# The second block's mixer in another order: ScalarE splits weights one unit ahead and empties whole tiles, GpSimd makes the rotation tables

## The chip, the core and the metric

One core of one Trainium2 chip. The metric is the device time of one execution in microseconds.

## The reference

Two transformer blocks of different kinds run one after the other on 256 tokens of width 1024, each with two layers, all in fp32. The change touches the mixer of the second block:

```python
h = rms_norm_2(x, attn_norm)
proj = h @ w_in                                     # 1024 x 5444
aq, ak, av, iq, ik, iw, bq, bk, bv, gates = split_cols(proj)
aq, ak, bq, bk = (apply_rope(rms_norm_2(., gain), cos, sin)) # per head of 64
iq = apply_rope(iq);  ik = apply_rope(rms_norm_2(ik, idx_k_norm))
ya = sparse_attention(aq, ak, av, iq, ik, iw, k_sel)         # 64 best keys by relu(iq.ik), 8 heads
yb = diff_attention(bq, bk, bv, lam)                         # 4 heads, p1 - lam * p2
merged = sigmoid(g_a) * (ya @ w_up_a) + sigmoid(g_b) * (yb @ w_up_b)
x = x + merged @ w_out
```

## The kernel before

Every large product runs as three passes of TensorE in a rounded fp32 format: w_hi with aT_hi, w_lo with aT_hi, w_hi with aT_lo (`three`, lines 1703 to 1705). Weights come in **units** of 128 x 2048 elements (1 MB). For each unit SP issues two loads into `raw` (line 402), ScalarE writes the rounded part `w_hi` (`split`, line 647) and VectorE the rest `w_lo` (line 1055). There are four slots: SP's load of unit u waits until VectorE has split unit u-4, ScalarE's split of u until TensorE has used u-4, and TensorE's use of u until VectorE has split it.

The second mixer's input projection has 11 **tiles** of 512 columns (the first has 324), listed in `WIN2`; tile n is units 2n and 2n+1, `P2_WIN + 2 * n + j` in the code, so that units 14 to 21 are `P2_WIN + 14` to `+ 21`. `full_k` runs a tile: for each unit, token half i = 0, then i = 1, four groups of three matmuls each, 16 groups a tile, numbered 0 to 15. `tile_half` is raised when the first token half of the tile is complete (group 11), `units_used` with the last group. The results are in two PSUM banks, one for each token half; the first four tiles alternate between banks 0, 1 and 2, 3, and from tile 4 on all use 0 and 1 (`BANK2`). A tile's first matmul in a bank waits in `free_banks` (line 2115) until the bank has been emptied. Tiles 0 to 6 are emptied by `evac`: ScalarE takes token half 0 (line 879), VectorE token half 1 (line 1444). Tiles 7 to 10 hold the gates, and VectorE adds their bias on the way out (`gate`, line 1454).

Between the groups TensorE does the attention's small work, at places written out by hand in the functions `beside_...` (lines 2191 to 2279): `turn` transposes the rotated projections (line 1822), `index_scores` and `pair_qk` are score products (lines 2135 and 2148), `pair_turn` transposes probabilities (line 2161), `diff_pv` and `sparse_pv` multiply them with the values (lines 2171 to 2173 and 2186). Pairs 0 to 3 are the differential heads, pairs 4 to 7 the sparse ones.

For each projection that is normalized per head, ScalarE squares (`head_squares`, line 888), VectorE sums (`head_sums`, line 1465), ScalarE takes roots (`head_roots`, line 901), VectorE the reciprocal (`head_scales`, line 1473), and GpSimd rotates (`rotate2`, lines 588 to 604), five times in a layer. The rotation reads tables `rg`, gain times cosine or sine, which VectorE makes in `gain_tables` (line 1422): those of the index key ahead of tile 0, the other four behind the first `head_sums`. `item` copies the transposed projections out of PSUM (lines 711 and 1128). For a pair k, VectorE masks the scores and takes their maximum (`masked`, line 1506), ScalarE takes exponentials (`exps`, line 919), VectorE scales (`probs`, lines 1514 to 1528), TensorE transposes, and `probs_turned` copies out (lines 930 and 1536). `index_relu` and `index_score` (lines 911 and 1482) make the score of the key selection, and 8 rounds of `best` (lines 1492 and 1495) find the 64 largest.

Each engine runs its part in the order in which the program writes it, and a wait holds everything behind it on that engine. For ScalarE the list starts at line 950, for VectorE at line 1569. SP issues the loads in the order of use; the layer's small parameters come ahead of unit 0, and 1 MB of gate bias is issued between units 3 and 4 (line 503), after the layer's input has been squared.

A range of SBUF is shared by both blocks and by the feed-forward layers (`proj1`, `proj2`, `gT_hi` and others, closed by `region_end`). It lies behind `att`, `ident`, `causal`, `score` and other small tensors.

## Time and profile before

| | us |
|---|---|
| median of 3 runs | 1948.23 (1947.63 to 1948.25) |
| the profiled execution's own time | 1948.37 |
| its span, first to last instruction | 1946.5 |
| second block, layer 0, tile 1's first matmul | 1109.24 |
| scores of pair 0 | 1160.93 |
| layer 0, VectorE's evacuation of tile 6 (half 1) | 1213.76 |
| layer 0, VectorE's last gate evacuation | 1279.00 |
| mean granted TensorE clock | 0.983 |

All times of a row count from the span's start. "Idle before" in brackets is how long the engine stood still, with the instruction that ended it. A clock of 1.00 is 2.4 GHz and 0.50 is 1.2 GHz.

### The profile page before, as it was taken

What the parts mean: (1) busy time and instruction counts of PE and PEld (TensorE: products, weight loads), DVE (VectorE), ACT (ScalarE), POOL (GpSimd) and SP (SyncE); (2) the same over time, 40 slices, a digit from 0 to 9 for tenths busy, and PEclk for the clock granted to TensorE, in tenths of its full rate; (3) what the DMA queues carried; (4) which work ended last, traced back from release to release, by engine and by line L of the source; (5) the groups of instructions that cost most, each with busy time, mean ns of one, the idle gap of its engine ahead of it and who ended that gap; (6) DMA issues with size and microseconds to landing.
All of it is one profiled execution on the core that took longest, in us unless ns stands there. A gap on an engine that the chain in (4) does not pass through costs nothing.

```text
span 1946.5 us, 25911 instructions
## 1 busy us (share of the span) xinstructions
PE 1828.4 (94%) x8739; PEld 1471.2 (76%) x8739; DVE 1137.0 (58%) x1710; ACT 924.2 (47%) x1249; POOL 174.7 (9%) x186
## 2 busy tenths in 40 slices
PE   6999999999989999999999787899999788899999
PEld 5888777788868887777888666687888666687887
DVE  5554677654445545776544587675554676665552
ACT  5444475544344434755443544544443544545441
POOL 0000110000000001100000183000000363000000
PEclk9999999999999999999999899999999999999999
DMA  7555362555446554625554343355545433355551
GB/s 230 182 194 203 130 193 66 173 185 201 158 153 191 184 210 132 190 70 173 176 202 165 147 155 109 109 174 180 187 173 187 153 130 109 130 195 161 184 190 69
DMA packets 221031, 316.49 MB, mean 163 GB/s; under 512 B 14048, under 2 KB 162160, under 8 KB 220656
## 3 DMA queue, kind: packets, MB, share of 16 engines
q1 hardware_dynamic: 220912, 315.02, 49.0%
q8 instruction: 60, 0.98, 0.2%
q14 instruction: 59, 0.48, 0.1%
HBM read 313.93 MB, written 1.05 MB: 162 GB/s over the span
## 4 chain that ended last, share of the span: by engine, by line
PE 75%; DVE 8%; ACT 7%; issue 4%; DVEq 4%; ACTq 1%; SPq 0%; DMA 0%
PE ps L1703 23%; PE ps L1705 23%; PE ps L1704 23%; ACT w_hi L647 3%; DVE w_lo L1055 2%; PE ps L1789 1%; ACT att L919 1%; DVEq L1515 1%; DVEq L1457 1%; ACT aT_hi L671 1%; PE ps L1713 1%; PE ps L1822 1%; DVE aT_lo L1075 1%; PE ps L1876 1%; PE ps L1852 1%
## 5 line engine op out<-in xcount | busy, mean ns | idle before, releaser
L1055 DVE TENSOR_TENSOR w_lo<-raw,w_hi 128x2048 fp32r<-128x2048 f32 x298 | 676.0, 2293 | 278.8 <-ACT w_hi L647 277.2
L1703 PE MATMUL ps<-w_hi,aT_hi 128*128 128x512 f32 (+2 forms) x1760 | 708.4, 403 | 53.7 <-DVE aT_lo L1075 31.7
L1705 PE MATMUL ps<-w_hi,aT_lo 128*128 128x512 f32 (+2 forms) x1760 | 687.1, 390 | 0.0
L1704 PE MATMUL ps<-w_lo,aT_hi 128*128 128x512 f32 (+2 forms) x1760 | 686.2, 390 | 0.0
L647 ACT ACTIVATE w_hi<-raw 128x2048 fp32r<-128x2048 f32 x298 | 557.2, 1906 | 171.1 <-PE ps L1705 166.9
L1703 PEld LDWEIGHTS ps<-w_hi,aT_hi 128*128 128x128 f32 x1760 | 334.3, 190 | 141.5 <-DVE aT_lo L1075 36.1
L1705 PEld LDWEIGHTS ps<-w_hi,aT_lo 128*128 128x128 f32 x1760 | 334.2, 190 | 70.0
L1704 PEld LDWEIGHTS ps<-w_lo,aT_hi 128*128 128x128 f32 x1760 | 335.2, 190 | 61.0
L686 ACT ACTIVATE att<-ps,rstd 128x256 f32<-128x256 f32 x132 | 55.3, 470 | 373.3 <-PE ps L1705 373.2
L1103 DVE SCALAR_TENSOR_TENSOR att<-ps,rstd,att 128x256 f32<-128x256 f32 x132 | 57.8, 480 | 275.6 <-ACT att L686 275.6
L1703 PE MATMUL ps<-w_hi,gT_hi 128*128 128x512 f32 x528 | 209.7, 397 | 0.0
L1705 PE MATMUL ps<-w_hi,gT_lo 128*128 128x512 f32 x528 | 208.5, 395 | 0.0
L1704 PE MATMUL ps<-w_lo,gT_hi 128*128 128x512 f32 x528 | 208.5, 395 | 0.0
L1705 PEld LDWEIGHTS ps<-w_hi,gT_lo 128*128 128x128 f32 x528 | 99.0, 187 | 24.4
L1703 PEld LDWEIGHTS ps<-w_hi,gT_hi 128*128 128x128 f32 x528 | 99.0, 187 | 23.5
L1704 PEld LDWEIGHTS ps<-w_lo,gT_hi 128*128 128x128 f32 x528 | 99.0, 188 | 23.4
L671 ACT ACTIVATE aT_hi<-ps,gain_l 128x128 fp32r<-128x128 f32 x160 | 43.4, 382 | 94.0 <-PE ps L1713 79.4
L1089 DVE SCALAR_TENSOR_TENSOR x<-ps,x 128x512 f32<-128x512 f32 x40 | 25.7, 685 | 86.6 <-PE ps L1705 86.6
L563 POOL COPY tt<-proj 128x512 f32<-128x512 f32 x4 | 4.5, 1162 | 679.8 <-DVE proj L1196 679.8
L1075 DVE SCALAR_TENSOR_TENSOR aT_lo<-ps,gain_l,aT_hi 128x128 fp32r<-128x128 f32 x160 | 43.7, 343 | 33.3 <-ACT aT_hi L671 33.3
L919 ACT ACTIVATE att<-att,neg_max 128x128 f32<-128x128 f32 x64 | 28.6, 448 | 72.3 <-DVE neg_max L1506 69.7
L749 ACT ACTIVATE att<-att,neg_max 128x128 f32<-128x128 f32 x96 | 43.0, 448 | 31.7 <-DVE neg_max L1225 27.5
(245 smaller groups left out, 1334.4 us busy)
## 6 DMA issues: line engine op xcount, KB each, us to landing
raw<-in_w_in SPq DMA_DIRECT2D x120, 512.0 KB, 4.4
raw<-in_w_ffn_gate SPq DMA_DIRECT2D x88, 512.0 KB, 4.2
raw<-in_w_ffn_up SPq DMA_DIRECT2D x88, 512.0 KB, 5.2
raw<-in_w_ffn_down SPq DMA_DIRECT2D x88, 512.0 KB, 4.4
raw<-in_w_ffn_in SPq DMA_DIRECT2D x88, 512.0 KB, 4.9
raw<-in_w_ffn_out SPq DMA_DIRECT2D x44, 512.0 KB, 4.4
raw<-in_w_out SPq DMA_DIRECT2D x32, 512.0 KB, 4.6
raw<-in_w_ck SPq DMA_DIRECT2D x8, 512.0 KB, 4.0
```

The source lines that it names most:

```text
L647: nc.scalar.activation(dst, src, ACT.Copy).then_inc(units_hi, 1)
L671: o = nc.scalar.activation(aT_hi[:, 4 * g + c, tok], bank[:, c], ACT.Copy, scale=gain_l[:, gain, 4 * g + c:4 * g + c + 1])
L686: o = nc.scalar.activation(sil[:, b % 2, i], ps[:, 2 * (b % 2) + i, 0:256], ACT.Silu, scale=rstd[:, i:i + 1])
L749: nc.scalar.activation(pair_p[:, k % 2, e, c:c + n], pair_p[:, k % 2, e, c:c + n], ACT.Exp, bias=pair_max[:, k % 2, e, i:i + 1], scale=-1. ...
L919: nc.scalar.activation(pair_p[:, k % 2, e, c:c + n], pair_p[:, k % 2, e, c:c + n], ACT.Exp, bias=pair_max[:, k % 2, e, i:i + 1], scale=-1. ...
L1055: V.tensor_tensor(o, a, h, ALU.subtract).then_inc(units_split, 1)
L1075: o = V.scalar_tensor_tensor(aT_lo[:, 4 * g + c, tok], bank[:, c], gain_l[:, gain, 4 * g + c:4 * g + c + 1], hi[:, c], ALU.mult, ALU.subtract)
L1089: o = V.scalar_tensor_tensor(xs, ps[:, src[i][n], :], scale, xs, ALU.mult, ALU.add)
L1103: o = V.scalar_tensor_tensor(gg[:, b % 2, i], ps[:, 2 * (b % 2) + i, 256:512], rstd[:, i:i + 1], sil[:, b % 2, i], ALU.mult, ALU.mult)
L1703: M(o, ah, wh, start=start, stop=False)
L1704: M(o, ah, wl, start=False, stop=False)
L1705: return M(o, al, wh, start=False, stop=stop)
```

## The change

The tensors from `att` to `factor` are allocated behind the shared region, so that this one follows `aT_lo`. GpSimd makes all five sets of rotation tables, ahead of its first rotation. ScalarE's `evac` takes both token halves, and one semaphore, `tile_done`, stands for a whole tile. ScalarE's splits of units 3 and on stand one place earlier in its list, the evacuation of tile 4 stands behind `exps(1)`, and VectorE's list follows the new order: splits one place earlier up to unit 16, `item(5)` ahead of a round of `best`. Behind unit 16's split VectorE's list stays as it was. TensorE's small work moves by a few groups in tiles 4 to 6.

```diff
@@
                 nc.gpsimd.tensor_tensor(a[:, i], a[:, i], lanes(scale[0][:, i, :], DH), ALU.mult)
             nc.gpsimd.drain()
+    pool.wait_ge(x_ready, 2 * 8)
+    pool.wait_ge(rope_sin, 2)
+    pool.wait_ge(params2_loaded, (l + 1) * 128)
+    for n in (2, 3, 4, 0, 1):
+        g = par2[:, 64 * n:64 * n + 64]
+        for k, (trig, half) in enumerate(((0, 0), (1, 1), (0, 1), (1, 0))):
+            nc.gpsimd.tensor_tensor(rg[:, n, k], cs2[:, trig],
+                                    heads(g[:, 32 * half:32 * half + 32], 2), ALU.mult)
+    nc.gpsimd.drain()
+
     for q, (n, c0, m0, g) in enumerate(HEAD_NORMS):
-        pool.wait_ge(proj_act, l * 7 + (12 + n + 1))
-        pool.wait_ge(proj_dve, l * 11 + (12 + n + 1))
+        pool.wait_ge(tile_done, l * 11 + (n + 1))
         if q == 0:
             rotate2(1536, 4, [cs2[:, 0], cs2[:, 1], cs2[:, 0], cs2[:, 1]])
         w = 1 if q == 0 else 8
@@
     B = l * STAGES2 + STAGES1 * L
     stage(B, 0)
     split(st, 1)
-    X, W, T = l * 2 + 7, l * 11 + 12, l * TJ2 + TJ1 * L
+    X, W, T = l * 2 + 7, l * 11, l * TJ2 + TJ1 * L
     J, O = l * PAIRS2 + PAIRS1 * L, l * 2 + 4 * L
     norm(X)
@@
         act.wait_ge(tile_half, l * 11 + (12 + n + 1))
         nc.scalar.activation(proj2[:, 0, c0:c0 + m], ps[:, BANK2[n][0], 0:m], ACT.Copy,
                              scale=rstd[:, 0:1]).then_inc(proj_act, 1)
+        act.wait_ge(units_used, st.used(P2_WIN + 2 * n + 1))
+        nc.scalar.activation(proj2[:, 1, c0:c0 + m], ps[:, BANK2[n][1], 0:m], ACT.Copy,
+                             scale=rstd[:, 1:2]).then_inc(tile_done, 1)
     def head_squares(q):
         n, c0, m0, _ = HEAD_NORMS[q]
         nc.scalar.drain()
-
-        act.wait_ge(proj_dve, W + (n + 1))
         if q != 0:
             nc.scalar.activation(squares2.rearrange("p (i n) -> p i n", i=2),
@@
             .then_inc(gates2_ready, 1)
     win_split(1, 0)
+    root(X)
     win_split(1, 1)
-    root(X)
+    win_split(2, 0)
     evac(0)
     head_squares(0)
+    head_roots(0)
     act.wait_ge(lam_sums, l + 1)
     nc.scalar.activation(lam[:, 0:2], lam[:, 0:2], ACT.Exp).then_inc(lam_exp, 1)
-    win_split(2, 0)
-    head_roots(0)
     win_split(2, 1)
+    win_split(3, 0)
     evac(1)
     head_squares(1)
-    win_split(3, 0)
+    win_split(3, 1)
     head_roots(1)
     item(0)
-    win_split(3, 1)
+    win_split(4, 0)
     index_relu(0)
     index_relu(1)
     evac(2)
     head_squares(2)
     index_relu(2)
     index_relu(3)
-    win_split(4, 0)
+    win_split(4, 1)
     head_roots(2)
     item(2)
-    win_split(4, 1)
+    win_split(5, 0)
     evac(3)
     head_squares(3)
     item(4)
-    win_split(5, 0)
+    win_split(5, 1)
     head_roots(3)
     exps(0)
-    win_split(5, 1)
+    win_split(6, 0)
+    exps(1)
     evac(4)
-    exps(1)
     probs_turned(0)
-    win_split(6, 0)
+    win_split(6, 1)
+    diff_out(0)
     exps(2)
-    diff_out(0)
     probs_turned(1)
-    win_split(6, 1)
+    split(st, P2_WIN + 14)
     exps(3)
     diff_out(1)
-    probs_turned(2)
     evac(5)
     head_squares(4)
+    probs_turned(2)
+    split(st, P2_WIN + 15)
+    head_roots(4)
     item(6)
-    split(st, P2_WIN + 14)
-    head_roots(4)
     diff_out(2)
     probs_turned(3)
-    split(st, P2_WIN + 15)
+    split(st, P2_WIN + 16)
     diff_out(3)
     evac(6)
     item(8)
-    split(st, P2_WIN + 16)
+    split(st, P2_WIN + 17)
     exps(4)
-    split(st, P2_WIN + 17)
+    split(st, P2_WIN + 18)
     exps(5)
-    split(st, P2_WIN + 18)
+    split(st, P2_WIN + 19)
     probs_turned(4)
     exps(6)
-    split(st, P2_WIN + 19)
     probs_turned(5)
+    split(st, P2_WIN + 20)
     exps(7)
+    sparse_hi(0)
+    split(st, P2_WIN + 21)
+    probs_turned(6)
     act.wait_ge(yb_ms, l + 1)
     nc.scalar.activation(ms[:, 0:8], ms[:, 0:8], ACT.Sqrt).then_inc(yb_root, 1)
-    split(st, P2_WIN + 20)
-    sparse_hi(0)
-    probs_turned(6)
-    act.wait_ge(proj_dve, W + 9)
+    split(st, P2_UP)
+    probs_turned(7)
+    act.wait_ge(tile_done, W + 9)
     gate(GATES2)
-    split(st, P2_WIN + 21)
-    probs_turned(7)
-    split(st, P2_UP)
+    split(st, P2_UP + 1)
     sparse_hi(1)
-    split(st, P2_UP + 1)
+    split(st, P2_UP + 2)
     stage(B + 4, parts=((0, 1), (1, 1)), banks=STAGE_BANKS_YB)
-    act.wait_ge(proj_dve, W + 11)
+    act.wait_ge(tile_done, W + 11)
     gate(GATES2 + DM)
-    split(st, P2_UP + 2)
     split(st, P2_UP + 3)
     split(st, P2_OUT)
@@
     stage(B, 0)
     split(st, 1)
-    def gain_tables(n):
-        g = par2[:, 64 * n:64 * n + 64]
-        for k, (trig, half) in enumerate(((0, 0), (1, 1), (0, 1), (1, 0))):
-            V.tensor_tensor(rg[:, n, k], cs2[:, trig],
-                            heads(g[:, 32 * half:32 * half + 32], 2), ALU.mult)
-
     dve.wait_ge(params2_loaded, (l + 1) * 128)
-    gain_tables(2)
     dl = par2[:, 448:704].rearrange("p (a b d) -> p a b d", a=2, b=2)
     V.tensor_tensor(score[:, 0:128].rearrange("p (a d) -> p a d", a=2), dl[:, :, 0, :], dl[:, :, 1, :],
@@
         .then_inc(lam_sums, 1)
     V.tensor_scalar(par2[:, 320:448], par2[:, 320:448], par2[:, 705:706], None, ALU.mult)
-    X, W, T = l * 2 + 7, l * 11 + 12, l * TJ2 + TJ1 * L
+    X, W, T = l * 2 + 7, l * 11, l * TJ2 + TJ1 * L
     J, O, A = l * PAIRS2 + PAIRS1 * L, l * 2 + 4 * L, l * 4 + (PAIRS1 * L - 4)
     def win_split(n, j):
         split(st, P2_WIN + 2 * n + j, 0, WIN2[n][1])
-
-    def evac(n):
-        c0, m = WIN2[n]
-        dve.wait_ge(units_used, st.used(P2_WIN + 2 * n + 1))
-        V.tensor_scalar(proj2[:, 1, c0:c0 + m], ps[:, BANK2[n][1], 0:m], rstd[:, 1:2], None,
-                        ALU.mult).then_inc(proj_dve, 1)
     def gate(n, i):
@@
             dve.wait_ge(units_used, st.used(P2_WIN + 2 * n + 1))
         V.scalar_tensor_tensor(proj2[:, i, c0:c0 + m], ps[:, BANK2[n][i], :], rstd[:, i:i + 1],
                                proj2[:, 1, c0:c0 + m], ALU.mult, ALU.add)\
-            .then_inc(proj_dve if i else gate_first, 1)
+            .then_inc(tile_done if i else gate_first, 1)
         V.drain()
@@
                 .then_inc(xn_ready, 1)
     win_split(1, 0)
+    norm(X)
     win_split(1, 1)
-    norm(X)
-    evac(0)
+    win_split(2, 0)
     head_sums(0)
-    for n in (3, 4, 0, 1):
-        gain_tables(n)
+    dve.wait_ge(tile_done, W + 1)
+    V.tensor_scalar(iw[:, 0, :], proj2[:, 0, 1856:1860], 0.5, None, ALU.mult)
+    V.tensor_scalar(iw[:, 1, :], proj2[:, 1, 1856:1860], 0.5, None, ALU.mult)
+    head_scales(0)
+    win_split(2, 1)
     dve.wait_ge(lam_exp, l + 1)
-
     V.tensor_tensor(lam[:, 2:3], lam[:, 1:2], lam[:, 0:1], ALU.subtract)
     V.drain()
     V.tensor_tensor(lam[:, 2:3], lam[:, 2:3], par2[:, 704:705], ALU.subtract)
-    V.tensor_scalar(iw[:, 0, :], proj2[:, 0, 1856:1860], 0.5, None, ALU.mult)
-    V.tensor_scalar(iw[:, 1, :], proj2[:, 1, 1856:1860], 0.5, None, ALU.mult)
-    win_split(2, 0)
-    head_scales(0)
-    win_split(2, 1)
-    evac(1)
+    win_split(3, 0)
     head_sums(1)
-    win_split(3, 0)
-    head_scales(1)
     item(1)
     win_split(3, 1)
+    head_scales(1)
+    win_split(4, 0)
     index_score(0)
     index_score(1)
-    evac(2)
+    index_score(2)
     head_sums(2)
-    index_score(2)
     index_score(3)
-    win_split(4, 0)
+    item(3)
+    win_split(4, 1)
     head_scales(2)
-    item(3)
     best(2)
-    win_split(4, 1)
-    evac(3)
+    win_split(5, 0)
     head_sums(3)
+    item(5)
     best(1)
-    item(5)
-    win_split(5, 0)
+    win_split(5, 1)
     head_scales(3)
     masked(0)
     best(1)
-    win_split(5, 1)
+    win_split(6, 0)
     probs(0)
     masked(1)
-    evac(4)
-    win_split(6, 0)
+    best(1)
+    win_split(6, 1)
     probs(1)
     masked(2)
-    best(1)
-    win_split(6, 1)
+    split(st, P2_WIN + 14)
     probs(2)
     masked(3)
-    evac(5)
+    best(1)
     head_sums(4)
+    split(st, P2_WIN + 15)
+    probs(3)
     item(7)
-    best(1)
-    probs(3)
     head_scales(4)
-    split(st, P2_WIN + 14)
     best(2)
-    split(st, P2_WIN + 15)
-    evac(6)
+    split(st, P2_WIN + 16)
     V.tensor_scalar(score[:, :], score[:, :], TAKEN, -NEG, ALU.not_equal, ALU.mult)
     V.drain()
     V.tensor_tensor(score[:, :], score[:, :], causal[:, :], ALU.add)
     V.drain()
     item(9)
-    split(st, P2_WIN + 16)
     masked(4)
     dve.wait_ge(bias_loaded, (l + 1) * 16)
@@
         def wait(i):
             if i == 1:
-                pe.wait_ge(proj_dve, W + m + 1)
+                pe.wait_ge(tile_done, W + m + 1)
             elif m < 7:
                 pe.wait_ge(proj_act, l * 7 + (12 + m + 1))
@@
             copied(3, 3)
             pe.wait_ge(idx_relu, l * 4 + 4)
             pair_qk(0)
-        if at == 12:
+        if at == 13:
             pair_qk(1)
         if at == 15:
             pair_turn(0)
     def beside_ak(at):
-        if at == 3:
+        if at == 4:
             pair_qk(2)
-            pe.wait_ge(proj_act, l * 7 + (12 + 5))
-            pe.wait_ge(proj_dve, W + 5)
+            pe.wait_ge(tile_done, W + 5)
             diff_pv(0)
-        if at == 6:
+        if at == 8:
             pair_turn(1)
-        if at == 10:
+        if at == 12:
             pair_qk(3)
             diff_pv(1)
-        if at == 13:
+
+    def beside_av(at):
+        if at == 0:
             pair_turn(2)
-
-    def beside_av(at):
-        if at == 2:
+        if at == 3:
             rotated(3)
             turn((6, 7))
             diff_pv(2)
-        if at == 5:
+        if at == 6:
             pair_turn(3)
-        if at == 10:
+        if at == 11:
             diff_pv(3)
@@
             pair_turn(4)
         if at == 10:
             pair_qk(6)
-            pe.wait_ge(proj_act, l * 7 + (12 + 7))
-            pe.wait_ge(proj_dve, W + 7)
+            pe.wait_ge(tile_done, W + 7)
             sparse_pv(4)
         if at == 14:
             pair_turn(5)
```

## Rows read from the trace of the kernel before

**Rows 1.** The page: busy time, share of the span and instructions of each engine.

```profile
PE 1828.4 (94%) x8739; PEld 1471.2 (76%) x8739; DVE 1137.0 (58%) x1710; ACT 924.2 (47%) x1249; POOL 174.7 (9%) x186
```

**Rows 2.** TensorE's waits, 1104 to 1180 us: releaser, us in total, times, longest.

```profile
PE ps L2148 <- DVE tt L1128: 4.1, 1, 4.1
PE ps L1703 <- DVE w_lo L1055: 3.4, 3, 1.9
PE ps L1822 <- POOLq L605: 2.3, 2, 1.4
PE ps L2161 <- DVE att L1528: 0.7, 1, 0.7
PE ps L1822 <- POOLq L617: 0.7, 1, 0.7
```

**Rows 3.** TensorE's waits, 1180 to 1215 us.

```profile
PE ps L2161 <- DVE att L1528: 7.5, 3, 3.1
PE ps L1703 <- ACT proj L879: 2.2, 1, 2.2
```

**Rows 4.** TensorE's waits, 1215 to 1280 us.

```profile
PE ps L1703 <- DVE proj L1454: 3.1, 2, 2.0
PE ps L2161 <- DVE att L1523: 2.1, 2, 1.9
PE ps L2186 <- DVE att L1536: 1.8, 1, 1.8
```

**Rows 5.** TensorE's waits in the second layer, 1531 to 1710 us.

```profile
PE ps L1703 <- DVE w_lo L1055: 3.5, 3, 2.0
```

**Rows 6.** Windows: length, busy PE, PEld, DVE, ACT, POOL, granted clock, DMA share, GB/s.

```profile
1104.00:1180.00 76.00, 65.12 (x308) 50.21 (x308) 63.06 (x114) 41.31 (x59) 48.76 (x39) 0.96 0.52 180
...
1215.00:1280.00 65.00, 58.01 (x289) 44.07 (x288) 39.62 (x80) 31.94 (x52) 3.54 (x4) 0.95 0.36 122
```

**Rows 7.** The same columns for one microsecond after the longest wait.

```profile
1163.00:1164.00 1.00, 1.00 (x4) 0.71 (x4) 1.00 (x5) 0.00 (x0) 1.00 (x1) 0.50 0.00 0
```

**Rows 8.** Timeline of TensorE, input tile 1: start, us, engine, line, instruction, idle before it.

```profile
1109.24 0.50 PE L1703 MATMUL ps<-w_hi,aT_hi 128*128 128x512 f32 x1 [0.29 <-DVE w_lo L1055]
...
1120.02 0.39 PE L1705 MATMUL ps<-w_hi,aT_lo 128*128 128x512 f32 x1
```

**Rows 9.** Timeline of GpSimd: first rotation, and a later one.

```profile
1112.72 0.74 POOL L588 TENSOR_TENSOR proj<-proj,cs 128x256 f32<-128x256 f32 x1 [269.57 <-DVE proj L1444]
...
1119.28 2.40 POOL L597 TENSOR_TENSOR proj<-proj 128x64 f32<-128x64 f32 x1
...
1124.83 0.40 POOL L616 COPY att<-proj 128x256 f32<-128x256 f32 x1
...
1195.36 1.29 POOL L588 TENSOR_TENSOR proj<-proj,rg 128x512 f32<-128x512 f32 x1 [27.36 <-ACT proj L879]
```

**Rows 10.** Timeline of VectorE: probabilities of pairs 0 and 1.

```profile
1171.65 0.75 DVE L1528 SCALAR_TENSOR_TENSOR att<-att,factor 128x128 f32<-128x128 f32 x2
...
1180.82 0.75 DVE L1528 SCALAR_TENSOR_TENSOR att<-att,factor 128x128 f32<-128x128 f32 x2
```

**Rows 11.** Timeline of VectorE: split of unit 17.

```profile
1226.84 2.29 DVE L1055 TENSOR_TENSOR w_lo<-raw,w_hi 128x2048 fp32r<-128x2048 f32 x1 [2.18 <-ACT w_hi L647]
```

**Rows 12.** Timeline of VectorE: rotation tables.

```profile
1113.39 5.29 DVE L1422 TENSOR_TENSOR rg<-cs,par 128x64 f32<-128x64 f32 x16
```

**Rows 13.** Timeline of VectorE: ahead of the first scores.

```profile
1157.11 1.22 DVE L1465 TENSOR_REDUCE ms<-proj 128x16 f32<-128x1024 f32 x1 [1.13 <-ACT proj L888]
...
1160.11 0.69 DVE L1128 TENSOR_SCALAR tt<-ps 128x512 f32<-128x512 f32 x1
```

**Rows 14.** Timeline of SP's DMA issues, and one window of DMA (columns as rows 6).

```profile
1105.49 18.99 SPq L402 DMA_DIRECT2D raw<-in_w_in  x11
...
1112.00:1113.00 1.00, 1.00 (x7) 0.80 (x6) 0.56 (x1) 0.87 (x4) 0.28 (x1) 1.00 1.04 399
```

**Rows 15.** Timeline of ScalarE: its half of tile 0's evacuation.

```profile
1112.02 0.53 ACT L879 ACTIVATE proj<-ps,rstd 128x324 f32<-128x324 f32 x1 [0.31 <-DVE rstd L1062]
```

More of the change, by code:

```diff
@@ L131, in build @@
         aT_lo = sb("aT_lo", [P, KC, SEQ], F32R)
-        att = sb("att", [P, 2304])
-        ident = sb("ident", [P, P])
-        causal = sb("causal", [P, 384])
-        cmask = sb("cmask", [P, 2, 16])
-        cvalid = sb("cvalid", [P, 2, 16])
-        head_mask = sb("head_mask", [P, 8])
-        gain_rows = sb("gain_rows", [80, P])
-        gain_cols = sb("gain_cols", [P, 80])
-        gain_l = sb("gain_l", [P, 3, KC])
-        ss = sb("ss", [P, 2])
-        rstd = sb("rstd", [P, 2])
-        rot1 = sb("rot1", [P, 2, 16])
-        neg_max = sb("neg_max", [P, 4, 2])
-        sums = sb("sums", [P, 4, 2])
-        with ExitStack() as r:
-            row_rot = r.enter_context(nc.sbuf_tensor("row_rot", [P, 4, 2, 8, 8], F32))
-        with ExitStack() as r:
-            score = r.enter_context(nc.sbuf_tensor("score", [P, 384], F32))
-        rot_end = sb("rot_end", [P, 512])
-        factor = sb("factor", [P, 4, 2])
         with ExitStack() as r:
@@ L177, in build @@
         region_end = sb("region_end", [P, 13800])
+        att = sb("att", [P, 2304])
+        ident = sb("ident", [P, P])
+        causal = sb("causal", [P, 384])
+        cmask = sb("cmask", [P, 2, 16])
+        cvalid = sb("cvalid", [P, 2, 16])
+        head_mask = sb("head_mask", [P, 8])
+        gain_rows = sb("gain_rows", [80, P])
+        gain_cols = sb("gain_cols", [P, 80])
+        gain_l = sb("gain_l", [P, 3, KC])
+        ss = sb("ss", [P, 2])
+        rstd = sb("rstd", [P, 2])
+        rot1 = sb("rot1", [P, 2, 16])
+        neg_max = sb("neg_max", [P, 4, 2])
+        sums = sb("sums", [P, 4, 2])
+        with ExitStack() as r:
+            row_rot = r.enter_context(nc.sbuf_tensor("row_rot", [P, 4, 2, 8, 8], F32))
+        with ExitStack() as r:
+            score = r.enter_context(nc.sbuf_tensor("score", [P, 384], F32))
+        rot_end = sb("rot_end", [P, 512])
+        factor = sb("factor", [P, 4, 2])
         with ExitStack() as r:
@@ L294, in build @@
         gate_first = sem("gate_first")
+        tile_done = sem("tile_done")
         rope_arg = sem("rope_arg")
@@ L2098, in _ @@
                 stage(x, x_ready, l * 2 + 7, 0)
-                T, W, A, D = l * TJ2 + TJ1 * L, l * 11 + 12, l * 5 + 10, l * 5 + 12
+                T, W, A, D = l * TJ2 + TJ1 * L, l * 11, l * 5 + 10, l * 5 + 12
                 B, J, O = l * STAGES2 + STAGES1 * L, l * PAIRS2 + PAIRS1 * L, l * 2 + 4 * L
```

## The prediction

> **What bounds the kernel now.** I read the page first, then TensorE's waits by stretch, then the timeline of all engines where they occur. TensorE is busy for 94% of the span [rows 1], so only what makes it stand still or slows its clock can be won. The change touches one stage, the second block's mixer, which runs twice. In the first layer, from 1104 to 1280 us, TensorE waits 11.2, 9.7 and 7.0 us in three stretches, 27.9 us in all [rows 2 to 4]; I call them early (to the first attention scores at 1160.9), middle (to the end of input tile 6, 1213.7) and late (tiles 7 to 10). The second layer has the same waits in the same places, as the three for weight splits, 3.5 us there and 3.4 here [rows 2, 5]. After the longer waits the granted clock falls to half, 1.2 for 2.4 GHz: it averages 0.96 early and 0.95 late [rows 6], and after the 4.10 us wait at 1156.8 TensorE still ran at half speed while busy in the row of 1163 [rows 7]. A full tile is 48 matmuls at 0.227 us, 10.9 us (first at 1109.24, last at 1120.02 plus 0.23) [rows 8].
>
> Three loops keep TensorE waiting. Early it is GpSimd's chain of rotations, the first of them 12.5 us long (1112.72 to 1125.23) [rows 9]; TensorE waited for three of them, 3.0 us in all [rows 2]. In the middle it is a loop through ScalarE and VectorE: scores masked, exponentials, ScalarE's split of a weight unit, VectorE's split of it, probabilities, the next scores. Probabilities are finished off at 1171.65 and again at 1180.82, so a turn takes 9.2 us [rows 10], while TensorE needs for a unit and what stands beside it 5.44 + about 3 us. Late, VectorE waits for ScalarE's split (2.18 us at 1226.84), since that stands behind the exponentials [rows 11].
>
> **Part 1, GpSimd makes the rotation tables.** 20 small multiplies a layer leave VectorE. 16 of them took 5.29 us behind the first head sums [rows 12]. GpSimd takes 0.74 us for a multiply four times as wide [rows 9], so 20 cost it at most 15 us. It does them before the first tile is ready, while it idles (269.57 us before its first rotation in layer 0 [rows 9]), so they lie off the path; in the code the parameters are loaded ahead of tile 0's weights. The unknown is whether they slow VectorE's 8 aT_lo at the head of layer 0, once: by nothing, or by one 0.33 us table instruction each (5.29 / 16), 3 us. I take 0, because those read PSUM and a single SBUF tensor, and the copy out of PSUM at 1160.11 took 0.69 us while GpSimd turned tile 3 [rows 13], no more than elsewhere. The address move of the shared region costs nothing: no instruction changes shape; a gain or loss would need a conflict that no row shows.
>
> **Part 2, early stretch.** ScalarE now splits units 3 and 4 ahead of evacuating tile 0. Unit 4's load goes out only at 1105.49, behind 1 MB of gate bias [rows 14], and at 0.36 to 0.40 MB per us [rows 14] the 2.1 MB are in at about 1112. So ScalarE splits it 1112 to 1113.9, then evacuates both halves (2 x 0.53 [rows 15]): GpSimd starts at 1115.0, not 1112.7. Worse, GpSimd's rotation stands still while VectorE splits. A 64-wide instruction took 2.40 us beside a split, where one of 256 took 0.74 and one of 512 took 1.29 without [rows 9]. Two such blocks lie in the 12.5 us, 8.4 without them. The rotation now runs beside the tail of unit 4's split (1.2), unit 5's (2.3) and unit 6's (2.3): 14 us, ending near 1129 instead of 1125.2. TensorE, which no longer waits 1.22 us for unit 4 and stands at that turn at 1122.8, waits 6 us (was 0.69). The second and third rotations follow 4 us later than before. What takes it back is the 4.10 us wait at 1156.8 [rows 2]: there the copy that the first scores need, at 1160.11, came behind VectorE's evacuation, ScalarE's squares (1.13 us of waiting), sums (1.22) and 1.8 us with a round of the top-k search in it [rows 13]. The change puts that copy ahead of the search round and takes the evacuation off VectorE. My walk brings the first scores to 1160.8, before 1160.9: **early, 0**. Ends: -6.6 (the 4.1 us wait and the 2.5 us lost to the slow clock behind it gone) and +4 (nothing absorbed).
>
> The Trainium skill (SBUF — State Buffer, Who interferes with whom) states that a VectorE instruction with two SBUF inputs and a GpSimd one that reads SBUF exclude each other for a whole instruction, and that one with a single SBUF input does not. The trace agrees on both: 2.40 us, and the unchanged 0.69 us copy. It speaks against splitting ahead, since each split moved into a rotation adds its full 2.3 us there; by a rule of shared bandwidth it would be about half.
>
> **Part 3, middle stretch.** ScalarE now empties both halves of tiles 4 and 5 behind exponentials 1 and 3, and the next tile needs the same banks. The loop's turn stays; between the two rows of [rows 10] the timeline has exponentials 2.2 us, ScalarE's split 1.9, VectorE's 2.3, probabilities 1.6 and masking, 0.4 to its first result. Walking it: TensorE waits at the first probabilities 2.9 (it arrives sooner, at full clock; was 0.72), at tile 5's start 2.8 (probabilities to masked 0.4, exponentials 2.2, evacuation 0.7, less the 0.5 of transposes), at the second and third none (were 2.05 and 2.36), since the turns were put 8 to 9 groups of 0.68 us apart instead of 7, at tile 6's start 4.8 (was 2.22 [rows 3]), at the fourth 0.9 (was 3.09): 11.4 us against 9.7 + 0.72. The 0.7 us of faster first scores and the low clock, one fall before and one or two after, about cancel: **middle, 0**, between -4 and +6.
>
> **Part 4, late stretch.** From the fifth pair's scores on, VectorE's order is as before, but ScalarE has every unit split beforehand: splits 17 to 21 move ahead of the exponentials. VectorE is busy for 39.6 of the 65 us [rows 6], which leaves room for a stretch of 56; what it lost was the wait for ScalarE [rows 11]. In the walk each of the five waits of [rows 4] goes (the nearest, the last probabilities, comes within 0.6 us of TensorE's need). Gone with them is the low clock: 0.05 of 65 us is 3.2 us, of which some 2.3 fell on a busy engine [rows 6]. **Late, -7.0 - 2.3 = -9.3**. Ends: -1.9 (only the last wait goes) and -10.2. What is late next is TensorE alone.
>
> Queues: SP's issues of weight units wait for VectorE's split four units back, all of which come at least as early except unit 3's (its split ends 2.3 us later, since the root goes ahead of it; TensorE needs it at 1114.7, it is there at 1113.7, and unit 7's load, queued behind it, is needed 10 us later). Table loads: the root for head 0 saves one and head 1 pays it, 1.28 us, hidden in TensorE's first wait. ScalarE's seven added evacuations are 4.6 us (7 at about 0.66) in an engine that is 47% busy [rows 1]; where it waits for a tile's end, the next split stands behind it, which part 3's walk holds. The upper projections and the rest keep their order and start 9 us sooner.
>
> **The sum.** 2 x (0 + 0 - 9.3) = -18.6 against the profiled execution's own 1948.37 us (span 1946.5; its 1.9 us around the span stay), which is 0.1 above the median shown: 1929.8, so 1930.
>
> **Rivals.**
> 1. *More is won* (0.15): the rotations suffer less than I walk and early gives -5 too, 2 x 14 = -28: 1920. For it: TensorE's early waits were small except the one that goes. Against: GpSimd's chain is serial.
> 2. *Little is won* (0.17): late waits turn into others, since exponentials still wait for masks (2.62 us [rows 11]) and VectorE has no slack; 2 x -2: 1944. Against it: VectorE is 61% busy there [rows 6].
> 3. *Slower* (0.18): evacuation behind the exponentials. At tiles 5 and 6 TensorE waits 2.8 and 4.8 us, each followed by some 5 us at half clock, 2 x 2.5, and the probabilities' waits do not shrink in return: +12.6 less 9.3 a layer, +6.6: 1955. It decides where the two waits with their clock exceed 9.3 us more than the middle gives back. For it: 2.22 us at 1195.26 was this very wait [rows 3], where ScalarE's half stood behind exponentials 3.
> 4. *Nothing changes* because loops trade place (0.06): 1948.
>
> **Chances.** My case 0.44. Faster by over 0.2% (3.9 us, about what a measurement of this kernel can tell): 0.44 + 0.15 + most of rival 2, 0.73. Within: 0.09. Slower: 0.18. Range: from rival 1 with the late end, 1914, to 1951, which leaves out the far part of rival 3 and little at the bottom. Where it is faster, its own range is 1916 to 1944.
>
> **What would show it.** Right: no wait of TensorE above 1 us after tile 6 and a late clock of 1.00; a wait of 4 to 6 us for GpSimd at the first turn; none at the first scores; waits for ScalarE's evacuation at the starts of tiles 5 and 6; tables on GpSimd long before the first rotation. Wrong: the first rotation ending before 1126 (part 2), the middle longer than 59 us (part 3), or waits for probabilities or gates in tiles 8 to 10 (part 4).

## The result and the profile after

The change brings 10.2 us: 1937.41 us (median of 5 runs, 1934.76 to 1937.53) against 1947.63 (5 runs), ratio 0.9945, interval 0.9931 to 0.996. The forecast was a gain of 18.6 us, to 1930, with a range of 1914 to 1951. The profiled execution is the fastest of the five (1934.76, span 1933.0), 2.6 us below the median; so what is added up from it is to be compared with 1948.37 - 1934.76 = 13.6 us and not with 10.2.

The page, its busy times (to be read against [rows 1]):

```profile
PE 1819.7 (94%) x8739; PEld 1477.6 (76%) x8739; DVE 1118.4 (58%) x1656; ACT 935.3 (48%) x1263; POOL 191.3 (10%) x226
```

TensorE has the same 8739 matmuls and is 8.7 us less busy. That is where the reading starts: something made the matmuls themselves quicker. And 6.5 us are won before the second block begins (its tile 0 starts at 1089.27 instead of 1095.8), where no instruction was changed.

TensorE's waits in the mixer of layer 0 after (1089 to 1270 us; for [rows 2 to 4]):

```profile
PE ps L2150 <- DVE att L1526: 7.4, 2, 4.5
PE ps L1692 <- ACT proj L889: 6.4, 2, 3.7
PE ps L1811 <- POOLq L627: 4.5, 1, 4.5
PE ps L1692 <- DVE aT_lo L1086: 4.1, 2, 3.5
PE ps L2150 <- DVE att L1521: 2.4, 1, 2.4
PE ps L1692 <- DVE w_lo L1066: 2.0, 1, 2.0
PE ps L2137 <- DVE tt L1139: 1.7, 1, 1.7
PE ps L1811 <- POOLq L606: 0.2, 1, 0.2
```

The 4.1 us for aT_lo and the 2.0 for w_lo lie ahead of tile 1. Windows of the same layer, early, middle and late (columns as [rows 6]), cut at tile 1's first matmul, the first scores, the turn in tile 7 (group 2), and the first upper projection:

```profile
1103.78:1155.22 51.44, 45.08 (x206) 35.64 (x204) 38.28 (x47) 32.14 (x39) 41.13 (x34) 0.93 0.58 198
1155.22:1212.61 57.39, 43.59 (x208) 33.55 (x209) 39.40 (x101) 27.93 (x56) 23.57 (x17) 0.91 0.36 118
1212.61:1269.67 57.06, 54.68 (x281) 42.43 (x280) 34.94 (x75) 32.19 (x52) 3.51 (x4) 0.97 0.35 119
```

The kernel before, cut at the same places:

```profile
1109.24:1160.93 51.69, 43.35 (x203) 33.75 (x204) 45.57 (x73) 27.58 (x35) 41.98 (x35) 0.98 0.58 201
1160.93:1215.61 54.68, 44.23 (x208) 33.64 (x209) 38.34 (x98) 25.18 (x52) 22.97 (x17) 0.92 0.35 111
1215.61:1278.80 63.19, 56.20 (x281) 42.63 (x280) 38.17 (x77) 31.94 (x52) 2.92 (x3) 0.95 0.36 121
```

Early -0.25, middle +2.7, late -6.1. Ahead of these windows tile 0 takes 14.5 us instead of 13.4, +1.1. From tile 0's start to the first upper projection with `ya` the mixer takes 180.4 us instead of 183.0, in layer 1 180.8 instead of 182.3: 4.1 us for both. The other 9.5 lie outside the code that the diff reorders. Windows of the same 40 us of a down projection in block 1, before and after:

```profile
160.00:200.00 40.00, 40.00 (x173) 32.12 (x172) 16.78 (x8) 14.23 (x8) 0.00 (x0) 1.00 0.66 225
```

```profile
160.00:200.00 40.00, 40.00 (x178) 33.15 (x177) 16.95 (x9) 14.83 (x8) 0.00 (x0) 1.00 0.67 230
```

Both have TensorE busy for the whole 40 us at a granted clock of 1.00, and 178 matmuls pass instead of 173. Measured from one matmul's start to the next one's, the mean is 227.0 ns instead of 233.3, in each of the six down projections (264 matmuls, 61.35 us for 62.95 in the first): 1.6 us each, 9.8 in all. Only the address of their stationary operands, `gT_hi` and `gT_lo`, is new: 147584 instead of 162400, bytes within a partition. Against it stand the upper projections, whose `ya_hi` and `ya_lo` moved from 205952 to 191136: the stretch from the first to the last of their 48 matmuls a layer, with others in between, takes 17.72 us instead of 17.44.

### The profile page after: what moved, and what is told of

The parts are those of the page before. It is cut to its first block, busy times and chain, and to the rows that moved or that the text cites. A ratio compares the mean times of both kernels' runs of the same rounds, so it can differ in the third digit from the quotient of the medians.

```text
span 1933.0 us, 25923 instructions
## 1 busy us (share of the span) xinstructions
PE 1819.7 (94%) x8739; PEld 1477.6 (76%) x8739; DVE 1118.4 (58%) x1656; ACT 935.3 (48%) x1263; POOL 191.3 (10%) x226
## 4 chain that ended last, share of the span: by engine, by line
PE 77%; issue 6%; DVE 6%; ACT 5%; DVEq 3%; POOL 2%; POOLq 1%; ACTq 0%; DMA 0%; SPq 0%
PE ps L1692 24%; PE ps L1694 23%; PE ps L1693 23%; ACT w_hi L657 2%; DVE w_lo L1066 2%; PE ps L1778 1%; POOL rg L614 1%; DVEq L1513 1%; PE ps L1811 1%; ACT aT_hi L681 1%; PE ps L1702 1%; PE ps L1865 1%; DVE att L1236 1%; DVE aT_lo L1086 1%; DVEq L1483 1%
## 5 line engine op out<-in xcount | busy, mean ns | idle before, releaser
L614 POOL TENSOR_TENSOR rg<-cs,par 128x64 f32<-128x64 f32 x40 | 17.2, 467 | 471.9 <-DVE x L1416 246.9
L759 ACT ACTIVATE att<-att,neg_max 128x128 f32<-128x128 f32 x96 | 42.9, 448 | 31.8 <-DVE neg_max L1236 27.5
```

Of the source, the lines that this page charges most:

```text
L614: nc.gpsimd.tensor_tensor(rg[:, n, k], cs2[:, trig], heads(g[:, 32 * half:32 * half + 32], 2), ALU.mult)
L759: nc.scalar.activation(pair_p[:, k % 2, e, c:c + n], pair_p[:, k % 2, e, c:c + n], ACT.Exp, bias=pair_max[:, k % 2, e, i:i + 1], scale=-1. ...
```

## The experiments

The times of one group share their runs of the kernel before (median 1948.71 for `e1` to `e4`, 1948.43 for `e5` and `e7` to `e9`, 1948.83 for `e6`, `e10` and `e11`, 1948.13 for `e12`; 1947.63 beside the kernel after). A difference between kernels of two groups can be off by about 1 us for that alone.

**The parts alone.** `e1_move` is the kernel before with only the allocation moved. `e2_order` is the kernel after with the allocation of before, so the order and the tables alone. `e3_pad` is the kernel before with one line added ahead of the shared region, `e4_after_pad` the kernel after with the same line:

```diff
+        pad = sb("pad", [P, 8])
```

> The kernel before with nothing but the allocation moved, so that the shared region starts at byte 147584 of a partition instead of 162400. Theory A: the move is worth some 10 us of the 10.2 measured, since in the profile after each of the six down projections took about 1.6 us less: 1938 us, and the mixer's waits stay as they were before (4.1 us at the first scores). Rival B: addresses are worth nothing and the down projections were faster by chance in that one profile: 1947.6.

> The kernel after with the old allocation: order and tables alone. Theory A: the order gives 2 to 3 us a layer, 1943 us, and the down projections are as slow as before (matmul pitch 233 ns). Rival B: the order gives everything, 1937.4.

> The kernel before with 32 unused bytes ahead of the shared region: the region starts at 162432, a multiple of 64, instead of 162400, which is 32 more than one. Theory A1, it is the start's remainder by 64 that matters: as e1_move, 1938, pitch 227 ns in the down projections. Rival A2, it is where the region lies as a whole: 1947.6, pitch 233.

> The kernel after with 32 unused bytes ahead of the region: it starts at 147616, 32 more than a multiple of 64. Theory A1: the down projections fall back to 233 ns a matmul, 1.6 us each, and the time to about 1947 less the order's 3 to 5, 1943 as e2_order. Rival A2: it stays at 1937.

Measured: `e1_move` 1940.02, ratio 0.9951 (0.9938 to 0.9965); `e2_order` 1947.46 (11 runs), 0.9994 (0.9985 to 1.0003); `e3_pad` 1939.05, 0.995 (0.9937 to 0.9964); `e4_after_pad` 1948.66 (11 runs), 0.9998 (0.9989 to 1.0007). So 32 unused bytes are worth as much as the whole change, and put in front of the change's own region they take its gain away. The order and the tables by themselves give 1.2 us with an interval that reaches from 2.9 to -0.6, where theory A had 4 to 6. The trace of `e2_order` shows why: its late stretches take 57.1 us in both layers, as in the kernel after, but its middle stretches 59.8 and 59.7, with the clock at 0.86, where the kernel before has 54.7 and 53.6. Its middle and late windows of layer 0:

```profile
1161.73:1221.49 59.76, 47.62 (x208) 36.47 (x209) 38.39 (x101) 27.92 (x56) 23.90 (x18) 0.86 0.37 122
1221.49:1278.63 57.14, 54.76 (x280) 42.43 (x279) 34.92 (x75) 32.20 (x52) 2.74 (x3) 0.97 0.33 111
```

So the order wins some 6 us a layer late and can give nearly all of it back in the middle. The window of the down projection in `e3_pad` shows the 178 matmuls:

```profile
160.00:200.00 40.00, 40.00 (x178) 33.13 (x177) 16.95 (x9) 14.99 (x8) 0.00 (x0) 1.00 0.67 234
```

**Which address.** Three kernels put unused bytes inside the shared region of the kernel after, so that the mixer's own tensors stay where they are:

```diff
 e9_lo_off
+            r.enter_context(nc.sbuf_tensor("gap", [P, 8], F32))
             gT_lo = r.enter_context(...)
 e10_plus64
+            r.enter_context(nc.sbuf_tensor("gap_hi", [P, 16], F32))
             gT_hi = r.enter_context(...)
+            rb("gap_y", [P, 24])
             ya_hi = rb("ya_hi", [P, 4, SEQ], F32R)
 e11_hi_off
+            r.enter_context(nc.sbuf_tensor("gap_hi", [P, 8], F32))
             gT_hi = r.enter_context(...)
+            r.enter_context(nc.sbuf_tensor("gap_lo", [P, 24], F32))
             gT_lo = r.enter_context(...)
```

(`e11_hi_off` has also 24 elements ahead of `ya_hi` and 8 ahead of `ya_lo`, which puts them at remainders 0 and 32 to 256 bytes.)

> The kernel after with 32 unused bytes between gT_hi and gT_lo: gT_hi still starts at a multiple of 64 bytes, gT_lo 32 bytes past one; the mixer's tensors keep their addresses. Theory (a stationary operand that starts 32 bytes past a multiple of 64 costs its own matmul about 19 ns): of the 264 matmuls of a down projection only the third with gT_lo are slow, so the mean distance between matmuls rises from 227.0 to about 229 ns, each projection by 0.5 us and the kernel by 3.3 us; the distance in front of or behind the gT_lo matmuls is 246 ns and the others stay at 227. Rival A (the lost time belongs to the pair of tensors or to VectorE's and ScalarE's writes of them, not to the matmul's own operand): all or none of the matmuls slow down, 10 us or 0. Rival B (every stationary operand off by 32 bytes loses 6.3 ns): the gT_lo matmuls take 233.3 ns, mean 229.1, the same sum but no 246 ns in the trace.

> The kernel after with 64 unused bytes ahead of gT_hi inside the shared region, so that gT_hi and gT_lo start 64 bytes past a multiple of 128 (still a multiple of 64), and 96 bytes ahead of ya_hi and ya_lo (the stationary operands of the upper projections), so that they start at a multiple of 128; the mixer's other tensors keep their addresses. Theory (the stationary operand has to start at a multiple of 128 bytes, as the runs so far have 233 ns for ya at 32 and at 64 past one and 227 at one): the down projections' mean distance between matmuls goes from 227 to 233 ns, 1.6 us each, and that of the upper projections from 233 to 227 ns. Rival (a multiple of 64 is enough, and the ya of the run with the padded address had another reason): down projections stay at 227.

> The kernel after with gT_hi 32 bytes past a multiple of 128 and gT_lo at one (the mirror of the run with gT_lo alone off), and ya_hi at a multiple of 128 with ya_lo 32 bytes past one. In that run, of three matmuls the one during which gT_lo is loaded came after 238 ns, the one after after 227 and the third after 235, 700 ns for the three as with both off. Theory (each change of stationary operand onto or away from an unaligned tensor costs, and a triple costs 700 ns as soon as any of its operands is off): 233 ns on the mean for both gT and ya. Rival A (only gT_lo's loads count): 227 for the down projections and 233 for the upper ones. Rival B (each unaligned load costs by itself 6.3 ns): 231.2 ns for gT, 229 for ya.

`e9_lo_off` took 1947.23 us (11 runs), the whole gain gone, and its six projections have 233.3 ns a matmul. The three matmuls of a group, from its timeline:

```profile
160.31 0.40 PE L1693 MATMUL ps<-w_hi,gT_hi 128*128 128x512 f32 x1
160.55 0.40 PE L1694 MATMUL ps<-w_lo,gT_hi 128*128 128x512 f32 x1
160.78 0.39 PE L1695 MATMUL ps<-w_hi,gT_lo 128*128 128x512 f32 x1
161.01 0.40 PE L1693 MATMUL ps<-w_hi,gT_hi 128*128 128x512 f32 x1
```

With `gT_lo` alone off, the group costs 19 ns more, 700 for 681, as much as with both off. My expectation of +3.3 us was wrong, and so was that of a price for each matmul. The lost time is spread: on the mean of the six projections 239 ns behind the second matmul, while the weight load of `gT_lo` runs, 232 behind the first, 228 behind the third. `e10_plus64` (one execution, 1946.33) gave 233.3 ns for `gT` at 64 bytes further, so a multiple of 64 is not what counts; and its `ya`, now at a multiple of 128, stayed at 17.74 us from the first to the last of the 48 matmuls, so a multiple of 128 is not either, which I had expected. `e11_hi_off` (one execution, 1945.84) gave 231.2 ns for `gT`, the value of its rival B, but 233.4 for `ya`, the value of the theory where rival B had 229. So neither holds as a whole, and 231.2 beside the mirror's 233.3 fits no simple sum. Windows of `e10_plus64` and of `e11_hi_off`:

```profile
160.00:200.00 40.00, 40.00 (x173) 32.25 (x172) 16.68 (x8) 14.21 (x8) 0.00 (x0) 1.00 0.65 223
```

```profile
160.00:200.00 40.00, 40.00 (x175) 32.50 (x174) 16.33 (x8) 14.60 (x8) 0.00 (x0) 1.00 0.67 229
```

Set side by side by the remainder of the address to 256, the runs agree. At 128: `gT` at 147584 and 162432, `aT_hi` and `aT_lo` in every kernel, `ya` at 205952, all 227. At 96, 160 and 192, and `ya` at 0: 232.6 to 233.4 on the mean of each run. Remainders 64 and 224 were not tried, and 32 only for `ya_lo` beside `ya_hi` at 0 (233.4). The weights, the moving operand, stood at remainder 128 in all kernels, so "128" and "the same as the weights" are not told apart.

**What the order gives, and what takes it back.** `e5_evac_first`, `e7_tables_dve` and `e8_evac0_first` are the kernel after with one part undone or turned round:

```diff
 e5_evac_first, ScalarE
+                evac(4)
                 exps(1)
-                evac(4)
@@
+                evac(5)
                 exps(3)
                 diff_out(1)
-                evac(5)
 e8_evac0_first, ScalarE
+                evac(0)
                 win_split(2, 0)
-                evac(0)
```

In `e7_tables_dve` the loop over the five tables is gone from GpSimd, and VectorE has `gain_tables(2)` at the head of the mixer and the other four behind `head_sums(0)`.

> The kernel after, with ScalarE's evacuation of tile 4 ahead of the exponentials of pair 1 and that of tile 5 ahead of those of pair 3. Theory (the middle stretch lost what the late one won, because the evacuation stands behind exponentials, rival 3's mechanism): the waits for the evacuation at the starts of tiles 5 and 6 (2.67 and 3.74 us) fall to under 1 us each and with them the half clock behind them, some 1 to 2 us a layer; 3 to 6 us a layer, so 6 to 12 us less than the kernel after, near 1928. Rival (the loop masked, exponentials, split, probabilities sets the middle; a wait taken away at the tiles' starts comes back at the next probabilities): the two waits go, those for the first and second probabilities grow by as much, the time stays within 2 us of 1937.

> The kernel after with the rotation tables back on VectorE at their old places (one table set at the head of the mixer, four behind the first head sums). Theory of the prediction (the tables are worth nothing, since what they hold up on VectorE is covered): within 2 us of the kernel after; 5.3 us more of VectorE's time behind the first head sums hold up the scales of head 0, so the first rotation ends up to 4 us later and TensorE's first wait for GpSimd, 4.50 us, grows by that if nothing covers it. Rival (the tables are what the new order needs): the first scores come 3 us or more later in each layer, 4 to 8 us slower than the kernel after.

> The kernel after with ScalarE's evacuation of tile 0 ahead of its split of unit 4 (a weight unit of tile 2), as before. Theory of part 2 of the prediction (the split in front delays the first rotation by some 2 us, TensorE waits for it at the first turn, and later work absorbs it): TensorE's wait at the first turn falls from 4.50 us to between 2 and 3, a wait for unit 4 of up to 1.2 us comes back, and the first scores come within 1 us of where they were: within 2 us of the kernel after. Rival (the 4.50 us are simply added to the early stretch): the stretch shortens by 2 us or more in each layer, 4 us or more faster in all.

`e7_tables_dve`: 1938.1 us, 0.7 slower than the kernel after and inside its expectation; the tables are worth nothing that can be told. `e8_evac0_first`: 1936.12, 1.3 faster. The wait at the first turn did not fall to 2 or 3 us: it is 4.85 in layer 0 and 3.89 in layer 1. It ends only 0.6 and 0.8 us sooner after tile 0's start than in the kernel after, and in layer 0 TensorE comes there 1 us sooner as well; the total fits, the path to it does not.

`e5_evac_first`: 1933.23, ratio 0.9916 (0.9903 to 0.993), 4.2 us less than the kernel after (4.9 less than `e7_tables_dve`, which was measured beside it), below the 6 to 12 expected. Its waits in layer 0:

```profile
PE ps L2150 <- DVE att L1526: 10.4, 4, 3.6
PE ps L1811 <- POOLq L627: 5.6, 1, 5.6
...
PE ps L2150 <- DVE att L1521: 2.4, 1, 2.4
```

The two waits for the evacuation, 6.4 us in all, are gone, and 3.0 us came back as waits for probabilities (10.4 for 7.4) and 1.1 as a longer wait at the first turn (5.6 for 4.5). The middle stretch takes 56.5 and 57.0 us, where the two passages of the kernel after have 57.4. Its timeline of ScalarE and VectorE shows why the waits stay:

```profile
1159.46 0.40 ACT L930 ACTIVATE att<-att,neg_max 128x128 f32<-128x128 f32 x1 [3.74 <-DVE neg_max L1504]
...
1161.85 1.92 ACT L657 ACTIVATE w_hi<-raw 128x2048 fp32r<-128x2048 f32 x1 [0.24 <-issue]
...
1163.79 2.29 DVE L1066 TENSOR_TENSOR w_lo<-raw,w_hi 128x2048 fp32r<-128x2048 f32 x1 [2.46 <-ACT w_hi L657]
...
1167.00 0.75 DVE L1526 SCALAR_TENSOR_TENSOR att<-att,factor 128x128 f32<-128x128 f32 x2
```

ScalarE idles 3.74 us, takes the exponentials, and only then splits the unit, for which VectorE waits 2.46 us with the probabilities behind it. `e6_splits_first` adds to `e5_evac_first`:

```diff
+                win_split(6, 0)
                 exps(0)
-                win_split(6, 0)
                 evac(4)
+                win_split(6, 1)
                 exps(1)
                 probs_turned(0)
-                win_split(6, 1)
                 diff_out(0)
+                split(st, P2_WIN + 14)
                 exps(2)
                 probs_turned(1)
-                split(st, P2_WIN + 14)
                 evac(5)
+                split(st, P2_WIN + 15)
                 exps(3)
                 diff_out(1)
                 head_squares(4)
                 probs_turned(2)
-                split(st, P2_WIN + 15)
```

> The kernel with the evacuations of tiles 4 and 5 first (1933.2), and in it ScalarE's splits of units 12, 13, 14 and 15 each ahead of the exponentials of pairs 0, 1, 2 and 3 instead of behind them. ScalarE idles 3.74, 2.70 and 3.74 us before exponentials 0, 1 and 3 while it waits for masks. Theory (each probabilities' wait comes from the chain exponentials, ScalarE's split 1.9, VectorE's split 2.3, probabilities, so taking ScalarE's split out of the chain takes 1.9 us off each turn): TensorE's four waits for the probabilities of pairs 0 to 3 (2.89, 0.71, 3.25, 3.58 us in layer 0) fall by about 2 us each, the middle stretch from 56.5 to 50 to 53 us: 7 to 12 us less in all, 1921 to 1926. Rival (VectorE is the bound of the middle: mask, split, probabilities in a fixed order, so its split only moves to where it delays the next mask): the waits change places, within 2 us of 1933.

Measured 1927.66, ratio 0.9888 (0.9871 to 0.9904), 5.6 us less than `e5_evac_first` where 7 to 12 were expected; the middle stretch takes 54.1 us in both layers. Two of the four waits for probabilities are gone, and a new one is there:

```profile
PE ps L2150 <- DVE att L1526: 6.5, 2, 3.4
PE ps L1811 <- POOLq L627: 4.7, 1, 4.7
PE ps L2160 <- ACT att L941: 2.6, 1, 2.6
PE ps L2150 <- DVE att L1521: 2.4, 1, 2.4
```

The 2.6 us are for turned probabilities that ScalarE copies behind the exponentials of pair 3. `e12_best` takes that away, and moves `ya` to remainder 128 (191360):

```diff
                 evac(5)
+                head_squares(4)
+                diff_out(1)
+                probs_turned(2)
                 split(st, P2_WIN + 15)
                 exps(3)
-                diff_out(1)
-                head_squares(4)
-                probs_turned(2)
@@
+            rb("gap_y", [P, 56])
             ya_hi = rb("ya_hi", [P, 4, SEQ], F32R)
```

> The kernel with evacuations and splits first (1927.7), and in it two things. (a) On ScalarE the squares of head norm 4, the output of pair 1 and the turned probabilities of pair 2 go ahead of the split of unit 15 and the exponentials of pair 3, behind which TensorE waited 2.64 us for the turned probabilities, VectorE 5.47 us for the squares and GpSimd 2.90. Theory (ScalarE's order is what still holds the middle stretch): the 2.64 us go, the fourth probabilities' wait (3.15 us) falls to under 2, the middle stretch goes from 54.1 to 50 to 52 us, 4 to 8 us in all: 1920 to 1924. Rival (exponentials 3 come 1.5 us later and the fourth probabilities with them): within 1.5 us of 1927.7. (b) ya_hi and ya_lo start at 191360, 384 past a multiple of 512. So far every stationary operand at 128 past a multiple of 512 (aT, gT of four kernels, ya of two) took 227 ns a matmul, and those at 96, 160, 192 and 256 past one took 233. If the rule is the remainder to 256, the upper projections' matmuls go from 233 to 227 ns (1.2 us in all); if it is the remainder to 512, they stay at 233.

Measured 1920.09 us (1919.03 to 1921.27), ratio 0.9857 (0.984 to 0.9873): 17.3 us less than the kernel after, and faster than both. Its middle window, and its upper projections' first and last matmul:

```profile
1155.05:1204.48 49.43, 42.94 (x209) 33.45 (x210) 39.22 (x101) 28.31 (x56) 25.95 (x18) 0.93 0.45 147
```

```profile
1261.59 0.39 PE L1693 MATMUL ps<-w_hi,ya_hi 128*128 128x512 f32 x1
...
1279.03 0.40 PE L1695 MATMUL ps<-w_hi,ya_lo 128*128 128x512 f32 x1
```

The middle takes 49.4 and 51.1 us. The fourth probabilities still cost a wait of 4.5 us, more than expected. The stretch of the upper projections is back at 17.44 us, with 227.1 ns from start to start of its `ya` matmuls, so the remainder to 256 counts and not that to 512; for 96 matmuls that is 0.6 us, and not the 1.2 I had expected.

## Why the prediction was right and wrong

**The address move (part 1)** is the first step that failed. It was sized at nothing, "no instruction changes shape; a gain or loss would need a conflict that no row shows", and it carries the gain: 9.8 us in the trace less 0.6 for the upper projections, and 8.7 and 9.7 us in `e1_move` and `e3_pad`. The kernel is faster mostly for another reason than the one given. The trace of the kernel before had the row that should have been asked for: the same matmul took 0.227 us with `aT` as its operand [rows 8] and 0.233 with `gT`, and of the two it is `gT` that the change moves.

**The tables (part 1)** at nothing: right. They take 7.66 us on GpSimd for 20, half of the 15 that bounded them, 16 us before its first rotation, and `e7_tables_dve` shows no difference that can be told:

```profile
1085.13 7.66 POOL L614 TENSOR_TENSOR rg<-cs,par 128x64 f32<-128x64 f32 x20 [246.90 <-DVE x L1416]
1108.88 2.01 POOL L589 TENSOR_TENSOR proj<-proj,cs 128x256 f32<-128x256 f32 x1 [16.09 <-ACT proj L892]
...
1114.88 2.19 POOL L589 TENSOR_TENSOR proj<-proj,rg 128x64 f32<-128x64 f32 x1
...
1117.56 2.19 POOL L595 TENSOR_TENSOR proj<-proj,rg 128x64 f32<-128x64 f32 x1 [0.21 <-issue]
...
1121.58 0.40 POOL L626 COPY att<-proj 128x256 f32<-128x256 f32 x1
```

**The early stretch (part 2)** at 0: right, -0.25; from 8.2 us after tile 0's start, where the prediction's stretch begins (1104), it is +0.8, since tile 0 takes 1.1 us longer. The forecast had nothing for tile 0; the experiments show 14.5 us for it also where its code is that of before (layer 1 of `e1_move` and `e3_pad`), and 13.4 in `e2_order`, so it is not shown to come from the change. The rotation takes 13.1 us (forecast 14; three instructions of 2.0 to 2.2 us beside VectorE's splits, where the kernel before had two of 2.4) and ends 3.3 us later against tile 0's start (forecast 3.8), TensorE waits 4.50 us for it (forecast 6), and the wait at the first scores falls from 4.10 to 1.67 us, where the prediction had none.

**The middle (part 3)** at 0: wrong by +2.7 us in layer 0 and +3.8 in layer 1, and by +5.1 and +6.1 in `e2_order`. The waits at the starts of tiles 5 and 6 came as walked, 2.67 and 3.74 us (forecast 2.8 and 4.8). Mis-sized were the first and the fourth probabilities, 4.53 and 2.87 us instead of 2.9 and 0.9. `e5_evac_first` and `e6_splits_first` show both causes. By the medians the evacuation behind the exponentials costs 4.2 us and ScalarE's split behind them another 5.6. By the profiled middle stretches the split costs 2.4 and 3.0 us, and the evacuation only 0.9 and 0.4 against the short passages of the kernel after, 3.3 and 2.7 against the long ones of `e2_order` (on these two courses see the last section). The mechanism of rival 3 was there, at a fifth to half of its 12.6 us a layer. The prediction also took the second layer to have the same waits as the first. It had not: TensorE waited 5.4 us there for what line 1528 writes and 8.2 in the first, so the middle to be kept was 53.6 us and not 54.7.

**The late stretch (part 4)** at -9.3: -6.1, and -6.5 in layer 1, and it is the steady part of the gain: the stretch takes 57.1 us in both layers of every kernel with the new order. Four of the five waits went as forecast; the last probabilities, which the walk had within 0.6 us of TensorE's need, still make it wait:

```profile
1256.07 1.01 PE L2150 MATMUL ps<-ident,att 128*128 128x128 f32 x6 [2.38 <-DVE att L1521]
```

and the clock is 0.97 instead of 1.00, two fifths of the rise from 0.95 that was counted on.

**The sum.** Order and tables together were put at -18.6 and gave -4.1 in the profiled execution and -1.2 by the medians of `e2_order`. 1937.4 lies inside the range, 7.4 above the forecast, and that it lies so near is luck: the address gave some 9 us that were put at nothing, and the order some 17 less than forecast. Of the three signs named for "wrong", the wait for probabilities in the gate tiles occurred. The first rotation did not end early: 1121.98, which is 1128.5 with the times shifted so that tile 0 starts as before. The middle stayed below the 59 us named in the profiled execution of the kernel after (57.4), but took 59.6 to 59.8 in `e2_order`, `e4_after_pad`, `e9_lo_off` and `e11_hi_off`, so this sign occurred too where the same order ran again.

## What to carry to other kernels

Compare the start-to-start time of the same matmul between its operands before anything else: where one tensor gives 233 ns and another 227 at full clock and no wait, try its address, since moving it costs one unused tensor. And where a change moves tensors as well as work, run each alone; here the order would have got the credit for the address. On an engine that serves both a loop and a stream of weights, put the stream's piece into the idle time ahead of the loop's, and the emptying of PSUM ahead of both; here the two moves gave 4.2 and 5.6 us.

## What the runs showed of the hardware

1. A fp32 matmul of 128x512 in the three-pass scheme takes 227.0 ns from start to start where its stationary operands begin 128 bytes past a multiple of 256 (the weights do so too), and 232.8 to 233.4 where both begin at 96, 160 or 192, or `gT_lo` alone at 160. `ya` gave 232.6 with both at 0 and 233.4 with `ya_hi` at 0 and `ya_lo` at 32; `gT` with `gT_hi` at 160 and `gT_lo` at 0 took 231.2. Why it is so remains open, and so does why `gT_lo` alone costs as much as both.

2. The same mixer code takes one of two courses. In the kernel after and in `e7_tables_dve`, `e8_evac0_first` and `e10_plus64`, which differ from it in little, a passage takes 179.9 to 180.8 us (five of eight) or 182.2 to 183.1 (three), and `e10_plus64` has one of each: 180.2 in layer 0 and 182.4 in layer 1. What all three long ones have and no short one has is a low clock behind the wait for the fourth probabilities: 115 to 120 us after tile 0's start the granted clock is 0.66 to 0.70 in the long ones and 1.00 in the short ones, though in `e10_plus64` TensorE waited less ahead of it in the long one (2.5 us and 2.9). That window in layers 0 and 1 of `e10_plus64`:

```profile
1210.95:1215.95 5.00, 5.00 (x27) 4.20 (x26) 4.63 (x12) 2.89 (x3) 2.68 (x3) 1.00 0.02 5
1635.51:1640.51 5.00, 5.00 (x18) 4.00 (x18) 4.25 (x14) 2.41 (x2) 2.05 (x2) 0.70 0.00 0
```

The two passages of `e10_plus64` differ already in tile 0, where the short one has the low clock. The same two layers, 10 to 15 us after tile 0's start:

```profile
1105.95:1110.95 5.00, 5.00 (x25) 4.91 (x24) 2.54 (x3) 3.44 (x4) 0.00 (x0) 0.66 0.98 357
1530.51:1535.51 5.00, 4.71 (x29) 4.18 (x28) 2.54 (x3) 3.44 (x4) 0.00 (x0) 1.00 0.97 353
```

Tile 0 takes 14.5 us in four of the five short passages and 13.4 in two of the three long ones. The courses differ by 2 us a layer that no edit explains, as large as what the order gives; the profiled execution of the kernel after has two short passages, and whether its four slower ones had long ones isn't shown. All passages of `e2_order`, `e4_after_pad`, `e9_lo_off` and `e11_hi_off` were long ones. What decides between them was not found.
